# A four-stage transformer block on one core: the attention's first quarter step of each slot goes ahead of the scan's step on VectorE and ScalarE

## The reference

```python
# group A, 8 heads x 64: a state S that is carried over the tokens (the scan)
sa = jnp.einsum('bhvk,bhk->bhv', S, -kk_t)
S = (S * w_t[:, :, None, :] + sa[..., None] * (kk_t * a_t)[:, :, None, :]
     + v_t[..., None] * k_t[:, :, None, :])
...
# group B, 8 heads x 64: stick-breaking attention, 128-query blocks (the sticks)
z = jnp.einsum('bhqd,bhkd->bhqk', qb, kb) * scale
log_beta = jax.nn.log_sigmoid(z)
log_1m = jnp.where(mask, log_beta - z, 0.0)
log_a = log_beta + lax.cumsum(log_1m, axis=3, reverse=True) - log_1m
A = jnp.where(mask, jnp.exp(log_a), 0.0)
outs.append(jnp.einsum('bhqk,bhkd->bhqd', A, vb))
...
y = jnp.concatenate([y_a, y_b], axis=-1).astype(h.dtype) @ w_out[l]
h = h + rmsnorm(y, g_post_mix[l])
m = rmsnorm(h, g_pre_ffn[l])
m = jnp.square(jax.nn.relu(m @ w_ffn_up[l])) @ w_ffn_down[l]
```

## The kernel before

| quarter | TensorE | ScalarE | VectorE |
|---|---|---|---|
| q0 | sums with `tri` (L1411 to L1413), task now-4 | exp of `a` (L1101), now-5 | `wsl` (L1223), now-3 |
| q1 | q.k into `zb` (L1435), now | copy of `zb` into `z` (L1108), now | `a` = z - sums (L1230), now-4, and clamp into `w` (L1236), now-1 |
| q2 | sums with `rest`, now-5 | exp and ln of `w` (L1121, L1123), now-1 | max into `w` (L1243), now-2 |
| q3 | product with v (L1462), now-6, every second task | rarely a copy | `wsh` (L1254), now-2 |

## Time and profile before

### The profile page before, as it was taken

One profiled execution on the slowest core, in us unless ns is written; L12 is line 12 of the kernel. 1 busy time (PEld: TensorE's weight loads), 2 busy tenths in 40 slices (PEclk: granted clock), 3 DMA queues, 4 the chain that ended last, 5 costly groups with the idle time before them and its releaser, 6 DMA issues. The chain is left out here.

```text
span 1616.7 us, 37201 instructions
## 1 busy us (share of the span) xinstructions
PE 1533.9 (95%) x15568; PEld 1287.1 (80%) x15568; DVE 1013.1 (63%) x1582; ACT 739.8 (46%) x1302; POOL 167.4 (10%) x225
## 2 busy tenths in 40 slices
PE   6999999998999999999779999999999999999997
PEld 6999999987777776777568877888888888888886
DVE  6142433426977778788657686555556666667666
ACT  6253534436777777777645453333333211111122
POOL 6132433321011010010000000000000000000000
PEclk9999999997999999999989999999999999999999
DMA  4334363565422323210245454323222422233335
GB/s 171 135 119 166 130 217 115 180 206 154 107 49 65 75 56 84 49 37 25 67 115 143 144 198 156 111 105 104 104 105 89 152 91 91 92 104 99 97 105 182
DMA packets 89964, 185.76 MB, mean 115 GB/s; under 512 B 7744, under 2 KB 48192, under 8 KB 89552
## 3 DMA queue, kind: packets, MB, share of 16 engines
q1 hardware_dynamic: 86064, 169.68, 34.0%
q10 hardware_dynamic: 3744, 13.85, 2.2%
HBM read 124.96 MB, written 57.49 MB: 113 GB/s over the span
## 5 line engine op out<-in xcount | busy, mean ns | idle before, releaser
L534 DVE TENSOR_TENSOR inproj_wl<-xn_raw,inproj_wh 128x1024 fp32r<-128x1024 f32 x27 | 33.0, 1222 | 150.4 <-ACT inproj_wh L425 150.4
L638 PE MATMUL inproj_acc<-xn_xh,inproj_wh 128*128 128x348 f32 (+1 forms) x384 | 126.5, 329 | 0.0
L638 PE MATMUL inproj_acc<-xn_xl,inproj_wh 128*128 128x348 f32 (+1 forms) x384 | 123.4, 321 | 0.0
L638 PE MATMUL inproj_acc<-xn_xh,inproj_wl 128*128 128x348 f32 (+1 forms) x384 | 123.3, 321 | 0.0
L2273 DVE TENSOR_TENSOR all_mh_f<-all_mh_f,tail_bank 128x512 f32<-128x512 f32 x112 | 76.8, 686 | 52.3 <-PE tail_bank L2427 50.4
L2273 DVE TENSOR_TENSOR all_ml_f<-all_ml_f,tail_bank 128x512 f32<-128x512 f32 x112 | 76.8, 686 | 51.9 <-PE tail_bank L2427 51.9
L2427 PE MATMUL tail_bank<-all_mh,tail_tl 128*128 128x512 f32 x256 | 100.9, 394 | 0.0
L2427 PE MATMUL tail_bank<-all_mh,tail_th 128*128 128x512 f32 x256 | 100.9, 394 | 0.0
L2427 PE MATMUL tail_bank<-all_ml,tail_th 128*128 128x512 f32 x256 | 100.9, 394 | 0.0
L2427 PE MATMUL tail_bank<-tail_th 128*128 128x512 f32 x256 | 99.8, 390 | 0.3 <-DVE tail_tl L2174 0.3
L2427 PE MATMUL tail_bank<-tail_tl,tail_th 128*128 128x512 f32 x256 | 99.8, 390 | 0.0
(11 more groups left out here) (323 smaller groups left out, 4398.3 us busy)
## 6 DMA issues: line engine op xcount, KB each, us to landing
tail_raw<-in_w_up SPq DMA_DIRECT2D x32, 512.0 KB, 4.5
u_scratch<-tail_c SPq DMA_DIRECT2D x64, 256.0 KB, 2.1
tail_raw_d<-in_w_down SPq DMA_DIRECT2D x32, 512.0 KB, 3.7
tail_raw_u<-u_scratch SPq DMA_DIRECT2D x32, 512.0 KB, 3.4
xn_raw<-in_w_in SPq DMA_DIRECT2D x28, 512.0 KB, 5.1
p_scratch<-inproj_out ACTq DMA_DIRECT2D x26, 520.0 KB, 2.8
chunk_scratch<-inproj_fields SPq DMA_DIRECT2D x4, 2720.0 KB, 9.5
mix_swp<-chunk_scratch SPq DMA_DIRECT2D x34, 256.0 KB, 5.3
```

Source lines behind the costliest of these rows:

```text
L534: w_low.done(dve.tensor_tensor(wl[s][:, :, :], raw[s][:, :, :], wh[s][:, :, :].bitcast(F32), ALU.subtract), "all")
L638: last = pe.matmul(acc[g][:, 0:size], w[s][:, kt, :], xx[:, kt, col:col + size], start=(kt == 0 and j == 0), stop=(kt == KD - 1 and j == 2))
```

## The change

`program` gets an argument `ahead`. With `ahead=1`, which ScalarE and VectorE now pass, one of the slot's quarters (the first) is issued in front of the scan's step of the slot, from slot 2 on, and the rest behind it as before. The number of quarters that are done at the end of each slot stays the same. TensorE passes nothing and keeps its order, as do SyncE and GpSimd.

```diff
--- before.py
+++ after.py
@@ -943,19 +943,25 @@
                     yield
             return lap
 
-        def program(lap, sticks):
+        def program(lap, sticks, ahead=0):
 
             slots = (CHUNKS + 1) * LAP_SLOTS
             quarters = 4 * (N + SB_LAG + 1)
             sticks = sticks()
             k = given = 0
             for n in range(CHUNKS + 1):
-                for _ in lap(n):
+                steps = lap(n)
+                for _ in range(LAP_SLOTS):
+                    for _ in range(ahead if k >= SB_START else 0):
+                        next(sticks, None)
+                    given += ahead if k >= SB_START else 0
+                    next(steps)
                     k += 1
                     due = max(0, k - SB_START) * quarters // (slots - SB_START)
                     for _ in range(due - given):
                         next(sticks)
                     given = due
+                assert next(steps, "end") == "end"
             assert k == slots and next(sticks, "end") == "end"
 
         @block.sync
@@ -1132,7 +1138,7 @@
                     if now - 1 in split_at:
                         high_k(*split_at[now - 1])
                     yield
-            program(halves(front, rear), sticks)
+            program(halves(front, rear), sticks, 1)
 
         @block.vector
         def _(dve):
```

## The result

| | before | after |
|---|---|---|
| median, 4 runs each | 1611.85 us (1610.99 to 1612.66) | 1623.61 us (1622.37 to 1624.08) |
| profiled execution, its own time | 1618.45 us | 1623.97 us |
| its span | 1616.7 us | 1622.3 us |
| mean granted TensorE clock | 0.982 | 0.985 |

The ratio of the times is 1.0072 (95% interval 1.0052 to 1.0092): 0.7% slower, 11.8 us between the medians, where 1625.0 was forecast. Two profiles of the kernel before differ by 6 us: the second (before_again in the experiments) took 1612.19 us, which is the median, so the surplus of the first was an accident of that execution. Rows are therefore compared with both, and the verdicts come from medians.

A forecast was written before the change was run, and what follows sets the result against it. The mixing stage was taken as bound by late scan steps, while sticks have slack. 13.5 + 8.1 - 5.8 - 2.3 - 1.9 + 1.0 = 12.6 us more gives a median of 1625, 0.8% slower; range 1605 to 1642.

The forecast's parts named there:

- q1 first: ScalarE's copy of `zb` ahead of its step waits for TensorE's q.k: 0.3 us in 27 slots, 8.1 us lost.
- q2 first: ScalarE's exp and ln ahead of its step wait for VectorE's clamp: 0.5 us in 27 slots, 13.5 us lost.
- q0 and q3 first: ScalarE's slots starting with early-ready q0 or mostly empty q3: costed at nothing.
- VectorE's waits shrink: TensorE's later waits for VectorE's `zi16` and `krk` (5.8 + 5.8) fall by half: 5.8 us given back.
- VectorE's lead helps ScalarE, 2.3, and stick waits, 1.9: TensorE waits less for ScalarE's steps in q0 and q3 slots, 2.3 us, and for sticks, 1.9 us.
- The start: Slot 2: the sticks' opening work ahead of `zi2` costs 1.0 us, from nothing to 2.45.
- The clock: TensorE's granted clock: no new fall from the mostly short delays; 0 to 5 us for the range.
- The surplus of the profiled execution: Its 5.92 us over the median of 1612.53 comes from the profiled run and stays.
- 27 slots of each kind: Slots 1 to 6 of each lap, where the next slot wants ScalarE's step: 27 with q2, 27 with q1.
- Faster: Rival: filling VectorE's idle time cuts TensorE's 18.6 us of waits by a third, giving 1606; chance 0.22.
- No change: Rival: slack of TensorE's next block swallows each delay, within 0.2%, 1612.5 us; chance 0.15.
- heavier: Rival: nothing given back, clock falls three times more, VectorE's steps late: 37.7 us more, 1650; chance 0.13.

The follow-up runs named there:

- before_again: The kernel before, unchanged, run once more for a second profile; its profiled execution took 1612.19 us.
- act_q1: Changed kernel, but ScalarE puts its first quarter ahead only where it is a q1 (copy of `zb`): 1616.09 us, ratio to before 1.0025.
- dve_only: Changed kernel, but only VectorE puts its first quarter ahead; ScalarE keeps its order of before: 1608.46 us, ratio to before 0.998.
- act_q2_alone: Kernel before, but ScalarE puts its first quarter ahead where it is a q2 (exp and ln); VectorE unchanged: 1617.46 us, ratio 1.004.
- opening_behind: Changed kernel, but both engines put the quarter ahead from slot 3 on instead of slot 2: 1623.53 us, ratio to before 1.0067.
- dve_late: Kernel before, but VectorE alone puts its first quarter ahead, from slot 3 on: 1607.08 us, ratio to before 0.9969.

## Why the prediction was right, and where its parts were not

**Direction, place and engine** were right. TensorE's waits for ScalarE's steps passed 20 us, the copies stood behind L1127 or L1114, the wait for z grew, VectorE's wait ahead of `nb` fell by half (from 9.3 us, by a third, against the second profile), and outside the stage nothing moved. The first matmul behind it, in the kernel before and then in the one after:

```profile
797.62 1.97 PE L2310 MATMUL tail_bank<-mixed_y,all_ones_bd 128*128 128x256 f32 x8 [1.57 <-PEq L863]
```

```profile
803.73 1.96 PE L2316 MATMUL tail_bank<-mixed_y,all_ones_bd 128*128 128x256 f32 x8 [1.57 <-PEq L863]
```

It comes 6.1 us later, and the span ends 5.6 later. In the second profile of before it starts at 792.84: 10.9 us from there, 11.8 at the end of the span. One thing that was to get no larger did: the waits for `zi16` and `krk`.

**The sum** came out at 12.6 for a measured 11.8. That it came so near is luck: its terms were off in both directions, and this cancelled. Each measured difference is good to about 3 us.

- *q1 first, 8.1*: measured 7.3 (act_q1 over dve_only). Right.
- *q2 first, 13.5*: measured 4.4, or 6.4 without VectorE's lead. This is the term that failed, by more than its error. The working fits its two places and fails as a mean for all. Without VectorE's lead it gives 0.74 and 0.60 us for the two slots (1.34 less the 0.74 already lost); in act_q2_alone they are 0.86 and 0.50 longer than before. But the starts of TensorE's blocks in that trace and in the two of before can be compared in 35 slots with a q2 first: 17 changed by less than 0.1 us, 17 grew by 10 to 11 us together, one shrank by 0.7, and a part of that growth is made up elsewhere. The two slots were of the dear sort. The second error is the lead itself, 0.35 us a slot; its rows stand behind this list.
- *q0 and q3 first, nothing*: 1.8 us, within what the intervals leave open.
- *VectorE's waits shrink, 5.8*: wrong. They grew, in the change and in dve_only. The argument that a step of VectorE comes no later after an idle moment leaves out the other moments, where up to 0.69 us stands in front of it. I named this price and costed it at nothing. Slot 0 of the seventh lap, the place shown for "fits", was such a moment: 0.45 us of waiting and the rounding stand in front, and the wait for `zi16` grew by 0.51 us.
- *VectorE's lead helps ScalarE, 2.3, and stick waits, 1.9*: the mechanism shows (the wait for the clamp 34.4 to 19.8). As time it is 3.2 us for VectorE alone, net of its own later steps. With ScalarE ahead too only 1.3 us of it are left (1.008 to 1.0072), which the runs don't tell from nothing.
- *The start, 1.0*: a wait of 3.1 to 4.0 us is there, but leaving it out gave 0.8 us (opening_behind) and 1.8 us (dve_late), neither beyond the intervals. Later waits of TensorE swallow most of it (`xx4` in slot 4 in opening_behind).
- *The clock, nothing*: right, 0.985 and 0.984 in the four runs after.
- *The surplus of the profiled execution "stays"*: it did not (0.4 us in the kernel after, none in before_again). The forecast of the median doesn't depend on it.
- *27 slots of each kind*: by `program` they are 26 with a q2 first and 28 with a q1, 0.2 us less in the sum.

**VectorE's lead in slot 2 of the seventh lap**, before and then after:

```profile
513.09 0.43 DVE L1254 TENSOR_SCALAR mix_wsh<-mix_w 128x512 fp32r<-128x512 f32 x1 [0.45 <-DVE mix_w L1243]
...
514.76 0.42 DVE L1236 TENSOR_SCALAR mix_w<-mix_z 128x512 f32<-128x512 f32 x1
```

```profile
512.50 0.68 DVE L1167 TENSOR_TENSOR mix_krk<-mix_bank,early_masks 128x512 f32<-128x512 f32 x1
...
514.75 0.42 DVE L1242 TENSOR_SCALAR mix_w<-mix_z 128x512 f32<-128x512 f32 x1
```

TensorE's block of slot 1 is 1.00 us later than before, and this clamp (L1236, L1242 now) is not: its lead is 1.01. One rounding less stands between `nb` and it (0.46 us), and `krk` now stands where VectorE waited 0.45 us for its own maximum; with small differences that is the whole. The pair behind it starts at 515.21 for 515.23. By these figures slot 2 costs 1.34 - 1.01 - 0.40, nothing, as measured. That is one place; how large the lead is in the others was not counted.

**The rivals.** "Faster" was right in direction for VectorE alone: dve_late is 5.8 us below before (ratio 0.9969). The rule of the Trainium skill cited there ("Perfetto Trace Analysis", "Identifying the Most-Contended Engine") names VectorE by the shares worked out there, and filling VectorE's idle time did gain, 0.3%. But the loss sat on the engine that is less busy than VectorE (311 of 432 us), since what counted there was the order of its work, not the amount. "No change" and "heavier" are out.

**What stays open**: whether VectorE's lead gains through fewer stick waits of TensorE alone, or also through the clock. The mean granted clock over the runs is 0.9862 in dve_only and 0.9856 in dve_late, against 0.9842 and 0.9839 for before beside them. Over all 174 timed runs of the three batches, within each kernel, a clock higher by 0.001 goes with 0.6 us less, so 0.002 would be about 1.2 of the 3.8 and 5.8 us between the medians. Which is cause there was not tested.

## What to carry to other kernels

Where engines run two streams in one fixed order, an item may go in front of the urgent one if its input was made long ago (not by the item right before it) by the same engine or comes from one that is ahead, and if the engine would be idle at that point. An item that waits for another engine in the same slot makes the urgent one wait too, and the engine's idle share says nothing about it: look at the releaser of the item and at the time the urgent one was ready. To cost such a move, follow several consecutive slots with everything that has shifted, take places from all over the stage, from more than one profile, and don't take the mean of neighbours as a price for all.

## What the runs showed of the hardware

One program, the same wait, and yet another clock. The longest wait for `krk`, TensorE of the kernel before in its first profile:

```profile
485.38 0.69 PE L1282 MATMUL mix_bank<-mix_xx,mix_nb 64*64 64x64 f32 x32 [2.38 <-DVE mix_krk L1161]
```

Behind it the clock was 0.57 of full speed. The same place in its second profile, and the windows around it:

```profile
483.81 0.69 PE L1282 MATMUL mix_bank<-mix_xx,mix_nb 64*64 64x64 f32 x32 [2.37 <-DVE mix_krk L1161]
```

```profile
484.00:488.00 4.00, 3.65 (x134) 3.15 (x133) 3.48 (x8) 1.91 (x5) 0.54 (x2) 1.00 0.00 0
488.00:492.00 4.00, 3.40 (x102) 2.75 (x93) 2.87 (x12) 3.70 (x10) 0.59 (x2) 1.00 0.02 6
```

Full speed, 2.4 GHz, behind a wait of the same length. So the length of the wait does not settle alone if the clock falls, and the price of a wait in clock can't be read from one profile. The difference shows in the times: over 17 runs the clock went from 0.980 to 0.988 and the times from 1608.57 to 1616.06 us, more than most of the effects in question here.

VectorE waits for itself too. Where the rounding L1254 follows the maximum L1243 at once, it starts 0.45 us after the maximum has ended (513.09 for 511.95 + 0.69). Over the mixing stage of the first profile before, these waits are 26 and sum to 11.4 us, about as much as its wait for TensorE ahead of `nb`. With `krk` between the two, as at 512.50 in the kernel after, the wait is gone there.
